# Six blocks of gate products of a streaming encoder layer on one core: one level of Strassen's scheme in place of plain products

## What is computed

```
split_points = np.cumsum(IN_WIDTHS)[:-1].tolist()
q_lat, c_kv, k_r, f_q, f_k, f_v, f_logit, m_q, g = jnp.split(h @ w_in, split_points, axis=-1)
gates = jax.nn.sigmoid(g.astype(jnp.float32)).astype(h.dtype).reshape(b, s, N_BRANCH, D_MODEL)
y = (gates[:, :, 0] * (o_mla.reshape(b, s, -1) @ w_br_mla)
     + gates[:, :, 1] * (o_fox.reshape(b, s, -1) @ w_br_fox)
     + gates[:, :, 2] * (o_mem.reshape(b, s, -1) @ w_br_mem))
return y @ w_out
```

## Time and profile before

| | us |
|---|---|
| median of 3 runs | 1150.53 (1148.98 to 1151.8) |
| profiled execution, its own time | 1151.25 |
| its span, first to last instruction | 1149.5 |
| PE busy | 1120.3 |
| PE weight loads busy (beside PE) | 638.7 |
| DVE busy | 479.1 |
| ACT busy | 208.8 |
| POOL busy | 53.3 |

### The profile page before, as it was taken

One profiled execution on the slowest core, in us unless ns is written; L12 is line 12 of the kernel. 1 busy time (PEld: TensorE's weight loads), 2 busy tenths in 40 slices (PEclk: granted clock), 3 DMA queues, 4 the chain that ended last, 5 costly groups with the idle time before them and its releaser, 6 DMA issues.

```text
span 1149.5 us, 16904 instructions
## 1 busy us (share of the span) xinstructions
PE 1120.3 (97%) x6218; PEld 638.7 (56%) x6218; DVE 479.1 (42%) x1356; ACT 208.8 (18%) x389; POOL 53.3 (5%) x59
## 2 busy tenths in 40 slices
PE   8999999999999999999999999999999999999995
PEld 4455446666666655466555555555555555555551
DVE  0141014445444333256454453453543544535425
ACT  0222125655333200010000101101101001011012
POOL 2100000000000000011000000000000000000000
PEclk9999999999999999999999999999999999999998
DMA  9522356214656479661699999999999999999981
GB/s 326 173 101 74 115 196 191 83 43 170 226 178 204 166 261 362 256 204 41 235 387 380 374 395 376 372 384 376 377 391 371 390 384 376 400 374 371 378 332 57
DMA packets 81586, 311.82 MB, mean 271 GB/s; under 512 B 11784, under 2 KB 24880, under 8 KB 55288
## 3 DMA queue, kind: packets, MB, share of 16 engines
q1 hardware_dynamic: 64704, 277.86, 61.8%
q0 software_dynamic: 5696, 15.47, 4.6%
q10 hardware_dynamic: 11136, 17.83, 4.5%
HBM read 305.09 MB, written 10.74 MB: 275 GB/s over the span
## 4 chain that ended last, share of the span: by engine, by line
PE 95%; DVE 3%; issue 1%; ACT 0%; DMA 0%; ACTq 0%; SPq 0%; DVEq 0%
PE ps_P L1210 20%; PE ps_P L953 11%; PE ps_V L1235 10%; PE ps_V L1224 10%; PE ps_P L861 8%; PE ps_V L1146 5%; PE ps_S L1224 5%; PE ps_P L869 4%; PE ps_V L1155 4%; PE ps_T L1199 3%; PE ps_T L852 2%; PE ps_S L962 2%; PE ps_P L994 1%; PE ps_V L1187 1%; PE ps_S L1217 1%; PE ps_V L920 1%
## 5 line engine op out<-in xcount | busy, mean ns | idle before, releaser
L1210 PE MATMUL ps_P<-arena,branch_out 128*64 128x256 f32 (+1 forms) x2176 | 233.6, 379 | 0.6 <-DVE branch_out L1831 0.6
L1210 PEld LDWEIGHTS ps_P<-arena,branch_out 128*64 128x64 f32 (+1 forms) x2176 | 151.2, 135 | 90.9 <-issue 19.2
L953 PE MATMUL ps_P<-xT,weight_ring 128*128 128x384 f32 x384 | 136.8, 491 | 0.0
L1837 DVE TENSOR_TENSOR branch_out<-branch_out,ps_P 128x256 f32<-128x256 f32 x33 | 13.9, 422 | 266.2 <-PE ps_P L1210 266.2
L1224 PE MATMUL ps_V<-weight_ring,branch_out 128*128 128x512 f32 x264 | 124.1, 592 | 0.0
L1406 ACT ACTIVATE weight_ring<-ps_V,merge 128x512 f32<-128x512 f32 x66 | 45.3, 687 | 427.6 <-PE ps_V L1235 421.4
L1235 PE MATMUL ps_V<-arena,branch_out 128*64 128x512 f32 (+1 forms) x544 | 120.6, 598 | 0.0
L1858 DVE TENSOR_TENSOR x_sb<-x_sb,ps_V 128x512 f32<-128x512 f32 x132 | 90.8, 688 | 17.3 <-PE ps_V L1224 17.3
L953 PEld LDWEIGHTS ps_P<-xT,weight_ring 128*128 128x128 f32 x384 | 68.9, 190 | 37.9 <-issue 2.1
L1224 PEld LDWEIGHTS ps_V<-weight_ring,branch_out 128*128 128x128 f32 x264 | 47.9, 191 | 47.3 <-issue 47.3
L1235 PEld LDWEIGHTS ps_V<-arena,branch_out 128*64 128x64 f32 (+1 forms) x544 | 34.8, 135 | 59.5 <-issue 58.9
(11 more groups left out here) (305 smaller groups left out, 1117.7 us busy)
## 6 DMA issues: line engine op xcount, KB each, us to landing
arena<-w_e_gate SPq DMA_DIRECT2D x68, 1024.0 KB, 8.5
arena<-w_e_up SPq DMA_DIRECT2D x68, 1024.0 KB
arena<-w_e_down SPq DMA_DIRECT2D x68, 1024.0 KB, 7.2
weight_ring<-w_in SPq DMA_DIRECT2D x12, 1024.0 KB, 8.8
weight_ring<-w_in ACTq DMA_DIRECT2D x8, 1024.0 KB, 8.0
gates<-arena ACTq DMA_DIRECT2D x24, 192.0 KB, 3.6
arena<-fox_k_t SPq DMA_DIRECT2D x8, 512.0 KB, 3.9
arena<-cache_fox_v SPq DMA_DIRECT2D x8, 512.0 KB, 4.8
```

The costliest lines, as they stand in the source:

```text
L953: last = mm(out[:, 0:T], slot[:, k % 4, m * P:(m + 1) * P], xT[:, k, :], start=(k == 0), stop=(k == KD - 1))
L1210: last = mm(bank[r:r + wide, 0:256], xgT[q][:, k, r:r + wide], w[h][:, k, :], start=(k == 0), stop=(k == KD - 1))
```

## The change

Two gate units (2 x 128 channels) are taken together, as a 2x2 block product: weights of two halves of the 1024 terms by two units, inputs of the same two halves by two halves of 192 tokens. In place of eight half-size block products there are seven, of sums of blocks (the Winograd form of Strassen's scheme). There are 12 such pairs. What it does:

- `plan()`: 84 entries `("W", i, r)` (pair i, product r from 0 to 6) in place of 96 pieces, spread in the same way over the same steps. After the sixth product (r = 5) stands `("weights", i + 1)`, DVE's sums for the next pair; `("weights", 0)` stands before `("prep", 0)`, and `("inputs",)`, DVE's sums of inputs, before the transposes of `mk`.
- PE: each product is four matmuls of 128x128 weights by 192 columns into one of two banks (half used), with waits for DVE's weight sums and for the reading of the product two before.
- DVE: four sums of inputs (768 columns each) once; per pair three sums of weights of 512 columns in one go, a fourth after the third product (partly in place in the ring), and seven sums that take results from PSUM into `gate_two`.
- ACT: copies the first product of each pair; one sigmoid over both units (768 columns) at the next pair's second product; one store of both.
- Arena: two buffers for results, four for input sums and two for weight sums lie where the cache buffers were; the cache buffers move over those of the prompt's mla and fox operands. So SP waits before the cache loads for the values of unit 15. The stores of fox_k get a semaphore of their own, on which DVE, SP and POOL wait.

The core of the diff:

```diff
+    s.append(("inputs",))
     s += [("T", "mk", j) for j in range(2)]
+    s.append(("weights", 0))
     s.append(("prep", 0))
     s.append(("V", "c", "p"))
 
-    pieces = [(n, k) for n in range(GATES) for k in range(0, KD, 2)]
+    pieces = [("W", i, r) for i in range(TWO) for r in range(7)]
+    n_pieces = len(pieces)
 
     def gate_piece():
-        n, k = pieces.pop(0)
-        s.append(("P", "g", n) if k == KD - 2 else ("gpiece", n, k))
+        st = pieces.pop(0)
+        s.append(st)
+        if st[2] == 5 and st[1] + 1 < TWO:
+            s.append(("weights", st[1] + 1))
...
-        while len(pieces) * (n_u + 4) > 4 * GATES * (n_u + 3 - n):
+        while len(pieces) * (n_u + 4) > n_pieces * (n_u + 3 - n):
...
+        Z = Space(R_A, a_cols, late)
+        gate_two = [None, Z.take(2, T)]
+        Z.take(512)
+        x_mix = [Z.take(4, HALF) for _ in range(4)]
+        gate_two[0] = Z.take(2, T)
+        w_sum, w_less = Z.take(4, P), Z.take(4, P)
...
+        B = Space(R_A, a_cols, prompt_at)
+        fkTc, mkTc, fvc, mvc = ([] for _ in range(4))
+        for i in range(2):
+            fkTc.append(B.take(4, 256))
+            mkTc.append(B.take(4, 256))
+            fvc.append(B.take(2, 512))
+            mvc.append(B.take(2, 512))
+            B.take(1024)
...
+        def gate_weights(i):
+
+            n, m = first_of["g"] + i // 2 * 2, i % 2 * 2
+            s0, s1 = wring[:, n % NW], wring[:, (n + 1) % NW]
+            a, b = slice(m * P, (m + 1) * P), slice((m + 1) * P, (m + 2) * P)
+            return s0[:, :, a], s1[:, :, a], s0[:, :, b], s1[:, :, b]
...
+                if b == 0:
+                    sp.wait_ge(done["V"], done_at("V", "o", 4 * H // 2 - 1))
...
-            def gate_products(n, k0):
-
-                st = ("P", "g", n)
-                out = bank(st) if k0 == 0 else ps["P"][pos_in[st] % 2]
-                slot = w_wait(first_of["g"] + (n // 4) * 2 + k0 // 4)
-                m = n % 4
-                for k in (k0, k0 + 1):
-                    last = mm(out[:, 0:T], slot[:, k % 4, m * P:(m + 1) * P], xT[:, k, :], start=(k == 0), stop=(k == KD - 1))
-                if k0 == KD - 2:
-                    last.then_inc(done["P"], 1)
+            def gate_product(i, r):
+
+                a11, a12, a21, a22 = gate_weights(i)
+                x_dif, x_all, x_end, x_low = x_mix
+                w, x = ((a11, xT[:, 0:4, 0:HALF]), (w_less, x_all), (a12, xT[:, 4:KD, 0:HALF]), (a21, x_end),
+                        (w_sum, x_dif), (a22, x_low), (a12, xT[:, 4:KD, HALF:T]))[r]
+                if r == 0:
+                    w_wait(first_of["g"] + i // 2 * 2)
+                    if i:
+                        pe.wait_ge(w_read, 7 * i - 1)
+                    else:
+                        pe.wait_ge(free["P"], done_at("P", "mv", 1))
+                elif r == 1:
+                    pe.wait_ge(x_mixed, 4)
+                    pe.wait_ge(w_mixed, 4 * i + 2)
+                    if i:
+                        pe.wait_ge(w_read, 7 * i)
+                elif r == 2:
+                    w_wait(first_of["g"] + i // 2 * 2 + 1)
+                    pe.wait_ge(w_copied, i + 1)
+                elif r == 3:
+                    pe.wait_ge(w_mixed, 4 * i + 3)
+                    pe.wait_ge(w_read, 7 * i + 1)
+                elif r == 4:
+                    pe.wait_ge(w_read, 7 * i + 2)
+                elif r == 5:
+                    pe.wait_ge(w_read, 7 * i + 3)
+                else:
+                    pe.wait_ge(w_mixed, 4 * i + 4)
+                    pe.wait_ge(w_read, 7 * i + 5)
+                for k in range(4):
+                    last = mm(gate_bank(i, r), w[:, k, :], x[:, k, :], start=(k == 0), stop=(k == 3))
+                last.then_inc(done["W"], 1)
...
+            def make_gates(i):
+
+                act.wait_ge(w_read, 7 * i + 7)
+                fn(gate_two[i % 2], gate_two[i % 2], ACT.Sigmoid).then_inc(gate_made, 1)
+                gates["made"] += 1
...
+                elif ring == "W":
+                    i, r = key
+                    if r == 0:
+                        if i >= 2:
+                            act.wait_ge(gates_stored, 16 * (i - 1))
+                        if i == 1:
+                            act.wait_ge(done["T"], done_at("T", "mk", 1))
+                            act.wait_ge(stored, 16 * PROJ_STORES)
+                        act.wait_ge(done["W"], done_at(*st))
+                        fn(gate_two[i % 2][:, 0, 0:HALF], gate_bank(i, r), ACT.Copy).then_inc(w_copied, 1)
+                    elif r == 1 and i:
+                        make_gates(i - 1)
+                    elif r == 6 and i % 2 and i // 2 + 2 < 6:
+                        w_load(act, first_of["g"] + i + 3)
+                        w_load(act, first_of["g"] + i + 4)
                 elif ring == "V" and key[0] == "b":
...
+                elif ring == "inputs":
+                    dve.wait_ge(done["P"], done_at("P", "qa", H - 1))
+                    dve.wait_ge(done["T"], done_at("T", "fk", TT - 1))
+                    dve.wait_ge(fk_stored, 32)
+                    x_dif, x_all, x_end, x_low = x_mix
+                    x11, x12, x21, x22 = (xT[:, k:k + 4, c:c + HALF] for k in (0, 4) for c in (0, HALF))
+                    V.tensor_tensor(x_dif, x12, x11, ALU.subtract).then_inc(x_mixed, 1)
+                    dve.wait_ge(x_mixed, 1)
+                    V.tensor_tensor(x_all, x22, x_dif, ALU.subtract).then_inc(x_mixed, 1)
+                    V.tensor_tensor(x_end, x22, x12, ALU.subtract).then_inc(x_mixed, 1)
+                    dve.wait_ge(x_mixed, 3)
+                    V.tensor_tensor(x_low, x21, x_all, ALU.subtract).then_inc(x_mixed, 1)
+                elif ring == "weights":
+                    i = key[0]
+                    a11, a12, a21, a22 = gate_weights(i)
+                    if i:
+                        dve.wait_ge(done["W"], done_at("W", i - 1, 4))
+                    for n in (0, 1):
+                        at = first_of["g"] + i // 2 * 2 + n
+                        dve.wait_ge(w_loaded[at % NW], loads_of(at))
+                    V.tensor_tensor(w_sum, a21, a22, ALU.add).then_inc(w_mixed, 1)
+                    dve.wait_ge(w_mixed, 4 * i + 1)
+                    V.tensor_tensor(w_less, w_sum, a11, ALU.subtract).then_inc(w_mixed, 1)
+                    V.tensor_tensor(a21, a11, a21, ALU.subtract).then_inc(w_mixed, 1)
+                elif ring == "W":
+                    i, r = key
+                    cells = gate_two[i % 2]
+                    c11, c12, c21, c22 = (cells[:, n, c:c + HALF] for n in range(2) for c in (0, HALF))
+                    if r == 0:
+                        continue
+                    dve.wait_ge(done["W"], done_at(*st))
+                    out = gate_bank(i, r)
+                    if r == 1:
+                        dve.wait_ge(w_copied, i + 1)
+                        V.tensor_tensor(c12, out, c11, ALU.add).then_inc(w_read, 1)
+                    elif r == 2:
+                        V.tensor_tensor(c11, out, c11, ALU.add).then_inc(w_read, 1)
+                        a12 = gate_weights(i)[1]
+                        dve.wait_ge(w_mixed, 4 * i + 3)
+                        V.tensor_tensor(a12, a12, w_less, ALU.subtract).then_inc(w_mixed, 1)
+                    elif r == 3:
+                        dve.wait_ge(w_read, 7 * i + 1)
+                        V.tensor_tensor(c21, out, c12, ALU.add).then_inc(w_read, 1)
+                    elif r == 4:
+                        dve.wait_ge(w_read, 7 * i + 3)
+                        V.tensor_tensor(c22, out, c21, ALU.add).then_inc(w_read, 1)
+                        V.tensor_tensor(c12, out, c12, ALU.add).then_inc(w_read, 1)
+                    elif r == 5:
+                        dve.wait_ge(w_read, 7 * i + 4)
+                        V.tensor_tensor(c21, out, c21, ALU.add).then_inc(w_read, 1)
+                    else:
+                        dve.wait_ge(w_read, 7 * i + 5)
+                        V.tensor_tensor(c12, out, c12, ALU.add).then_inc(w_read, 1)
```

More of the change, by code:

```diff
@@ L76 @@
 GATES = 24
+TWO = GATES // 2
+HALF = T // 2
 MERGE = [(cb, br, m) for cb in range(2) for br in range(3) for m in range(4)]
@@ L272, in build @@
     pos_in = {}
-    count = {"P": 0, "S": 0, "T": 0, "V": 0}
+    count = {"P": 0, "S": 0, "T": 0, "V": 0, "W": 0}
     for st in PLAN:
@@ L354, in build @@
         fv_tok = A.take(TT, 512)
-        kcat = A.take(H, 256)
         qabsS = A.take(NB, P)
-        qcat = A.take(H, 256)
-        v_mla = A.take(2, 512)
         qrS = A.take(NB, P)
@@ L362, in build @@
         w_kv = A.take(1024)
+        prompt_at = A.at
+        kcat = A.take(H, 256)
+        qcat = A.take(H, 256)
+        v_mla = A.take(2, 512)
+        fqA = A.take(H, 256)
+        fkA = A.take(H, 256)
         late = A.at
+        lat_all = A.take(1280)
+        lat_raw = lat_all[:, 0:TT * 424].rearrange("p (j c) -> p j c", j=TT)
         w_q = A.take(2, 768)
-        lat_raw = A.take(TT, 424)
```

(43 more changed lines are left out.)

49 lines of the change are left out of this document (22 added, 27 removed).

## The result

The changed kernel takes 1151.43 us (median of 20 runs, 1150.35 to 1153.61), the kernel before 1149.30 (20 runs, 1148.77 to 1151.96): ratio 1.0019, 95% interval 1.0013 to 1.0025. The changed kernel is 2.1 us slower instead: less than the 0.3% that the forecast calls the edge of no change, but the interval leaves out 1, so the direction is clear.

A forecast was written before the change was run, and what follows sets the result against it. PE's queue was taken as the bound, busy 97% of the span. Products -14.6, start +2.0, waits +6.9 and catching up +2.0 summed to -3.7 us: from 1151.25 to 1147.5 us, range 1141 to 1166.

The forecast's parts named there:

- Products: Gate products on PE: 384 records become 672 of 192 columns at 0.1625 us; gain 14.6 us (16.3 to loss of 3.9).
- Rival 2: Gate products on PE: weight loads bound the narrow products, 0.190 us per record; +14.8 us, 1166.0; chance 0.05.
- DVE's work: Gate stage on DVE: 4.4 us of new sums per pair, 53 us over 12 pairs; DVE some 68% busy.
- The start: First three weight sums on DVE delay preparation of unit 0 and PE's first scores; loss 2.0 us (0 to 3).
- The waits in the steps: PE's scores wait for DVE's release behind result and weight sums: loss 6.9 us, plus 2.0 for DVE catching up.
- the backlog: DVE about 2 us behind after three weight sums, catching up within two steps; 0.25 for each of eight, 2.0 us.
- the trio's price: Three weight sums on DVE after a sixth product, delaying the scores' release: 4.1 of the 6.9 us of gaps.
- Rival 3: DVE late only behind the groups of three weight sums, no catching up, 0.160 per record: -10.2 us, 1141; chance 0.15.
- rival 4: More gaps than the plan shows in the first 16 units, release still early: +2 to +8 us, 1155; chance 0.13.
- Rival 1: Scores' release on DVE comes late, behind result and weight sums: 27 us instead of 6.9; +16.4, 1167.7; chance 0.17.
- The step that failed: In the gate stage PE's queue is the bound, so time saved there shortens the end equally; MoE shift passed on whole.
- The base: Starting time of the sum: the profiled execution's 1151.25 us, 0.7 above the median of three runs, 1150.53.

The follow-up runs named there:

- a_skip32: Changed kernel with 32 waits (16 instructions) inside the jumped-over block of PE's program, never executed; 1147.41 us, ratio to the kernel before 0.9985.
- the last kernel: Changed kernel with first weight sums ahead of memory keys' copies, normalizing and release ahead of products, 16 unexecuted instructions in the jumped-over block; 1137.35 us, ratio to before 0.9896.

## Where the forecast held and where it failed

- **Products** held: 0.1625 us per record. From the start of each product's record to PE's next start, the trace adds up to 125.8 us before, 111.5 in a_skip32 and 111.2 in the last kernel: 14.3 to 14.6 us gone. In the last kernel the stage is 233.6 - 221.16 = 12.4 shorter, and PE's idle time in it 2.1 longer (2.40 for 0.34). The forecast's reason for the figure has a slip: 384 columns at 2.4 GHz are 0.160 us, while the record of 384 advances PE by 0.3225, two clocks a column. The figure for 192 columns is half of 0.320 plus the same 2.5 ns, so it stands. Rival 2 (loads bound) fell. PE's load time rose from 638.7 to 678.7 us, and PE's queue still got shorter. The Trainium skill, Perfetto Trace Analysis, section Identifying the Most-Contended Engine, names the load's busy share (beside the share of peak arithmetic) as the measure of TensorE's headroom; here that share rose while the work got less, so the advance of the records decides.
- **DVE's work** held: sums of 192 columns 347 to 358 ns, of 512 681 to 691, 148 us busy in the stage, 65%, for the forecast's 158 and 68%.
- **The start** held as a wait: 1.83 us for 2.0. Not in the sum: the clock that can drop behind it, 1.7 us.
- **The waits in the steps**, 6.9 + 2.0 = 8.9, held as a sum: without the drop the stage is 227.7, and 233.6 - 14.6 = 219.0, so they were 8.7. Counted from start to start, PE's records other than products take 8.3 us more than before in a_skip32 (116.1 for 107.8). Only a part of it stands in the profile as idle time: 227.69 - 222.67 = 5.0 us in this row (columns of the earlier trace rows), where before had 0.3; the rest lies inside the durations of records. The waits ahead of scores inside the stage that the view of waits lists are 3.5 us, half of them with "issue" as their cause, the longest 1.1; the forecast wanted near 7, released by DVE.

```profile
166.23:393.92 227.69, 222.67 (x1846) 186.68 (x1847) 148.14 (x493) 76.20 (x173) 0.00 (x0) 1.00 0.47 160
```

  The division was off. To the release belong 4.9 and not 6.9, which leaves 3.8 and not 2.0 for what the forecast called the backlog (1.6 of it the normalizing); and the trio's price doesn't depend on standing ahead of the release: whatever follows it on DVE is late. Rival 3 (no backlog, 0.160 per record) fell with these numbers, and rival 4 (more gaps than the plan shows) has no room in a sum of 8.7 for 8.9.
- **Rival 1** (late release, 27 us) fell. A wait of 0.99 shows the early release directly: the release (L1848, at 193.7) passes as the second sum of the trio starts, and PE goes on before the third, which stands ahead of the release in the program. In order of time:

```profile
193.69 0.69 DVE L1796 TENSOR_TENSOR arena<-arena,weight_ring 128x512 f32<-128x512 f32 x1
193.87 0.67 PE L917 MATMUL ps_S<-arena 128*128 128x256 f32 x2 [0.99 <-DVEq L1848]
194.30 0.68 DVE L1797 TENSOR_TENSOR weight_ring<-weight_ring 128x512 f32<-128x512 f32 x1
```

  PE's scores were running when that third sum began. The Trainium skill, PSUM — Partial Sum Buffer, section Engine vs sequencer instructions, has it that such an increment waits for dispatch and not for completion; these rows agree.
- **At the merge** the forecast is met when no clock drop intervenes: 398.06 - 393.92 = 4.1 us (a_skip32) for 3.7. In the profile of the changed kernel it is 2.4, since the drop at the start took 1.7.
- **The step that failed** is the first one: "a microsecond off PE's queue is a microsecond off the end", with the shift of the MoE stage "passed on whole". The saving was passed on up to the last pair (2.45 of 2.44 us), and lost behind it. There the change met something that is no work at all, and that the sum has at nothing: the tail is 4.0 us longer in the profiles (29.1 for 25.1). Of these 2.43 are the hole, 1.4 a larger loss to the lower clock, 0.2 a longer wait ahead of the last products. So 4.0 - 2.45 makes the changed kernel's span 1.5 us longer (1151.0 for 1149.5) in place of 3.7 shorter. The forecast listed the MoE stage as a place that would prove it wrong, but had priced nothing there.
- **The base** hid a part: the profiled execution of before, 1151.25, has the drop in the tail, and lies 2.0 above the median of 20 runs, 1149.3. Against that median the forecast's sum gives 1145.6. The kernel with the hole removed has 1147.4 to 1147.9, and 1145.8 in its best runs, those of a profile with no drop at either place. The rest, 1.8 to 2.3, is likely the drop in the tail, which these runs would have more often than those of before: the profiled execution of a_skip32 has it (25.25) and, with 1147.32, lies at its median, while that of before has it and lies 2.0 above. For the medians it is not shown.

## What to carry to other kernels

A saving on the bounding engine has to be followed to the last instruction: read the last 30 us of the trace too, and after any change of a program's length look for "issue" holes behind a jump before blaming the work; a few unexecuted instructions in the block jumped over settle it in one run. When work is given to an engine that also releases buffers, put the release and whatever the critical engine needs next ahead of it in program order; moving only the largest piece just changes who waits. A short idle time of TensorE at the head of a dense stretch may cost as much again through its clock (here 1.7 us behind 2.64 of idle, in three profiles of seven).

## What the runs showed of the hardware

- A hole of 1.94 to 2.67 us in PE's issue behind the first record after a taken jump, decided by where the program's length puts the code: it stands in all eight profiles where the first of the last products is instruction 8,146 or 8,658 of PE's compiled program, and in none of the six where it is 8,045 or 8,674.
- The granted clock fell, on the same program, in some executions and not in others: behind 2.64 us of idle three times of seven (1.7 us), in the last products three times of six where there is no hole (1.7 to 1.9 us).
- 202 satisfied waits at PE's head put its first product at 13.49 and not 5.41: 8.1 us later, at least 0.04 for each wait and at most 0.07 (13.49/202), since the first of them pass while PE would wait for its input anyway. 32 of them did not show: the first product started at 5.47.
